# Compressed attention branch: two heads in one transposition and one weighted sum, with a block diagonal value matrix

## The chip, the cores and the metric

One core of a Trainium2 chip runs the whole kernel in one launch. The metric is the device time of one execution in microseconds (us). PE is TensorE, DVE VectorE, ACT ScalarE, Pool GpSimd, and SP is SyncE, which here only issues transfers.

## The reference

The kernel computes one decoder layer for 1024 tokens of width 1024 in float32: a normalised mixer with three families of heads (4 NSA heads, 8 sliding window heads with sinks, 4 stick-breaking heads), an output projection, and a gated feed-forward part. The change touches the first of three branches of the NSA heads, the compressed one:

```python
def nsa_compress(kv, pos, w1, b1, w2):          # 63 compressed keys or values of 64
    idx = jnp.arange(nc)[:, None] * 16 + jnp.arange(32)[None]
    blocks = (kv[:, idx] + pos).reshape(b, nc, 32 * d)
    return jax.nn.silu(blocks @ w1 + b1) @ w2

# per block of 128 queries, 4 heads, one shared set of compressed keys kc and values vc
lc = einsum('bhqd,bcd->bhqc', qb, kc) * scale + bias_tab[t5_bucket(dist_c)]
pc = masked_softmax(lc, dist_c >= 0)
o_c = einsum('bhqc,bcd->bhqd', pc, vc)
...
return g[0] * o_cmp + g[1] * o_slc + g[2] * o_win
```

In the sizes used every selection takes in all blocks, so the selected branch is full causal attention.

## The kernel before

The kernel runs in stages: projections, attention, output projection, feed-forward. Attention is cut into jobs of 128 queries by 4 heads: 8 stick-breaking jobs (`sb`), 16 sliding window jobs (`swa`), and then for each of 8 query blocks n a compressed (`cmp`), a window (`win`) and a selected (`slc`) job. "Compressed job n" below is that of block n; it sees L = 8n + 7 compressed keys, 7 to 63.

A job runs in these steps. `scores` (L980, L988): PE multiplies queries by keys, each number as a high and a low part. `logits` (L1390): DVE adds the bias, negates, and keeps the minimum of each row in `neg`. `softmax` (L1186): ACT takes the exponential; the rows lie in `rows_sb`, `rows_swa`, or `rows_nsa[kind]`, 128 queries on the partitions. `turn` (L1015): PE transposes 128 queries by up to 128 keys of each of the 4 heads into one PSUM bank. `keep` (L1216 on ACT or L1420 on DVE, whichever the plan finds free) copies that bank to one of three slots of `tw`. `weigh` (L1037): PE multiplies the turned weights by the values, 66 columns for each head (64 values and two ones, whose result is the sum of the weights), into bank `SUMS`. `combine` (L1443, L1446, L1450, L1456): DVE divides, multiplies by the gate and adds to the mix. The next job's first `weigh` waits for it. After a block's last job come squares on ACT (L1236), their mean on DVE (L1462), the root on Pool (L809), `norm_mix` on DVE (L1470), and the transposition of the mix (L1004).

In this float32 form each product is two PE instructions, a transposition is one. For a compressed job there are 4 transpositions of 128 x L and 4 products of L x 66; `VC` holds the values, 64 partitions of 66.

The order of all engines' work in attention is written out by `plan_attention`: a list scheduler that is given a cost for each step, what it needs and an age, and emits a fixed order for each engine. At run time semaphores guard each need. The last projection pieces (`piece`, L899) lie between the attention jobs, and the last one ends just before the first compressed logits, because `rows_cmp` shares its room with operands of the pieces. The gain of the NSA norm, `g_n`, has a tile of its own and is loaded by `("strip", 4)` (L746) after the last piece. Output weights are loaded and split (L1250, L1480) during attention.

## Time and profile before

| | before |
|---|---|
| median of 3 runs | 1280.15 us |
| lowest run | 1279.1 us |
| profiled execution | 1279.56 us |
| its span | 1277.8 us |
| PE busy | 1247.4 us (98%) |
| DVE busy | 869.9 us (68%) |
| ACT busy | 603.4 us (47%) |
| Pool busy | 251.4 us (20%) |
| mean granted TensorE clock | 0.990 |

The span runs from the first to the last instruction of the profiled execution; 1.8 us of its time lie around it. Busy shares are means over stages with different limits. PE's ends are modelled, so a busy PE may still have gaps.

### The profile page before, as it was taken

How to read it: one execution, taken by the hardware profiler on the slowest of the kernel's cores; microseconds unless marked ns; L12 is line 12 of the kernel's file. 1: busy time of each engine (PE TensorE's matmuls, PEld its weight loads, DVE VectorE, ACT ScalarE, POOL GpSimd, SP SyncE). 2: the span in 40 equal slices, each digit the busy share in tenths (PEclk: the TensorE clock that was granted, in tenths of full speed). 3: DMA queues.
4: the chain of work that ended last, by engine and by line, in shares of the span. 5: the costliest groups of instructions: out<-in, count | busy, mean ns of one | idle time of the engine just before them, and what ended most of it. 6: DMA issues, size and time to landing. Idle time of an engine off the chain costs nothing.

```text
span 1277.8 us, 19230 instructions
## 1 busy us (share of the span) xinstructions
PE 1247.4 (98%) x6792; PEld 1069.3 (84%) x6792; DVE 869.9 (68%) x1609; ACT 603.4 (47%) x1142; POOL 251.4 (20%) x198
## 2 busy tenths in 40 slices
PE   9999999999999999999999999999999999999997
PEld 7898878789989888888788888888888887788886
DVE  6323788768868666355976656656756659969875
ACT  6432677756657555343643333333333336544441
POOL 5230111110000000011001112111212137607113
PEclk9999999999979999999999999999999999999999
DMA  6303421147632000222312232233232367372433
GB/s 229 117 1 117 116 51 51 30 118 178 147 120 67 18 18 6 75 86 99 132 42 96 100 119 80 86 124 124 91 115 93 118 210 266 110 228 89 135 138 132
DMA packets 67172, 136.45 MB, mean 107 GB/s; under 512 B 8663, under 2 KB 27359, under 8 KB 67076
## 3 DMA queue, kind: packets, MB, share of 16 engines
q1 hardware_dynamic: 67076, 135.22, 33.9%
q8 instruction: 55, 0.90, 0.3%
q14 instruction: 41, 0.34, 0.1%
HBM read 89.81 MB, written 28.60 MB: 93 GB/s over the span
## 4 chain that ended last, share of the span: by engine, by line
PE 81%; DVE 9%; issue 4%; ACT 2%; POOL 1%; DMA 1%; SPq 1%; DVEq 0%; POOLq 0%; ACTq 0%
PE ps L2392 33%; PE ps L2422 13%; PE ps L1037 7%; PE ps L2336 6%; PE ps L1015 4%; PE ps L880 4%; PE ps L825 3%; PE ps L899 3%; PE ps L980 2%; PE ps L988 2%; DVE ring L1406 2%; PE ps L914 1%; DVE m_rows_sb L1413 1%; DMA m_qs<-m_qn 1%; DVE ring L1398 1%
## 5 line engine op out<-in xcount | busy, mean ns | idle before, releaser
L2392 PE MATMUL ps<-f_topH,f_W 128*128 128x512 f32 x704 | 220.4, 389 | 0.0
L2392 PEld LDWEIGHTS ps<-f_topH,f_W 128*128 128x128 f32 x704 | 132.2, 188 | 27.4
L2392 PE MATMUL ps<-f_topL,f_W 128*128 128x512 f32 x352 | 136.9, 389 | 0.0
L1037 PE MATMUL ps<-V,m_tw 128*128 128x66 f32 (+1 forms) x1056 | 130.2, 273 | 1.1 <-DVE m_mix_n L1450 1.1
L1037 PEld LDWEIGHTS ps<-V,m_tw 128*128 128x128 f32 x1056 | 127.7, 193 | 2.6 <-DVE m_mix_n L1450 1.5
L2422 PE MATMUL ps<-f_headH,f_W 128*128 128x512 f32 x408 | 128.5, 391 | 1.2 <-DVE QT L2217 1.1
L2392 PE MATMUL ps<-f_headH,f_W 128*128 128x512 f32 x352 | 116.1, 393 | 2.4 <-DVE f_p1a L2189 2.4
L2182 DVE TENSOR_TENSOR f_W<-f_scr,f_W 128x512 fp32r<-128x512 f32 x88 | 62.0, 708 | 79.0 <-ACT f_W L1967 78.9
L2182 DVE TENSOR_TENSOR f_W<-ring,f_W 128x512 fp32r<-128x512 f32 (+1 forms) x84 | 77.3, 929 | 42.5 <-ACT f_W L1967 42.4
L2422 PEld LDWEIGHTS ps<-f_headH,f_W 128*128 128x128 f32 x408 | 76.6, 188 | 18.0 <-issue 2.0
L1216 ACT COPY m_tw<-ps 128x512 f32<-128x512 f32 (+4 forms) x93 | 52.8, 583 | 66.3 <-PE ps L1015 36.1
L2392 PEld LDWEIGHTS ps<-f_headH,f_W 128*128 128x128 f32 x352 | 66.9, 190 | 16.6 <-issue 2.8
L2422 PE MATMUL ps<-f_headL,f_W 128*128 128x512 f32 x204 | 79.4, 389 | 0.0
L2392 PEld LDWEIGHTS ps<-f_topL,f_W 128*128 128x128 f32 x352 | 66.1, 188 | 13.7
L809 POOL TENSOR_TENSOR m_rs<-m_ms,m_mhalf 128x1 f32<-128x1 f32 x24 | 15.6, 648 | 277.2 <-DVE m_ms L1462 277.2
L2422 PE MATMUL ps<-f_b22H,f_W 128*128 128x512 f32 x208 | 66.9, 393 | 2.7 <-DVE QT L2217 1.9
L2392 PE MATMUL ps<-f_headL,f_W 128*128 128x512 f32 x176 | 69.2, 393 | 0.0
L2217 DVE TENSOR_TENSOR QT<-ps,QT 128x512 f32<-128x512 f32 x67 | 45.8, 684 | 28.9 <-PE ps L2422 28.8
L899 PE MATMUL ps<-m_hH,m_wH 128*128 128x512 f32 x144 | 59.6, 414 | 4.9 <-ACT QT L1118 4.8
L805 POOL TENSOR_TENSOR QT<-QT 128x512 f32<-128x512 f32 x24 | 34.8, 1462 | 148.6 <-ACT QT L1118 140.1
L2336 PE MATMUL ps<-o_w,o_mH 128*128 128x512 f32 x224 | 60.5, 392 | 0.0
L2392 PE MATMUL ps<-f_b22H,f_W 128*128 128x512 f32 x176 | 57.7, 389 | 0.0
(285 smaller groups left out, 2887.2 us busy)
## 6 DMA issues: line engine op xcount, KB each, us to landing
act_pairs<-QT SPq DMA_DIRECT2D x77, 256.0 KB, 4.1
f_stage<-act_pairs SPq DMA_DIRECT2D x77, 256.0 KB, 2.7
m_qs<-m_qn SPq DMA_DIRECT2D x128, 128.0 KB, 2.4
ring<-in_ffn_w_up SPq DMA_DIRECT2D x22, 512.0 KB, 3.7
ring<-in_ffn_w_gate SPq DMA_DIRECT2D x19, 512.0 KB, 4.6
ring<-in_w_in_tiles SPq DMA_DIRECT2D x9, 512.0 KB, 3.7
ring<-in_nsa_phi_w SPq DMA_DIRECT2D x8, 512.0 KB, 4.7
ring<-in_w_out SPq DMA_DIRECT2D x8, 512.0 KB, 5.0
```

Of the source, the lines that this page charges most:

```text
L805: pool.tensor_tensor(half_room(h), half_room(h), scale_row[:, half_cols(h)], ALU.mult).then_inc(half_scaled, 1)
L825: return pe.matmul(ps[:, h, :], w[:, k % W_ITEMS, (h // 2) * P:(h // 2 + 1) * P], a[:, k, half_cols(h)], start=first, stop=last)
L880: ins = pe.matmul(ps[:, b + a, 0:VW_HALF], h[:, k, tok], wv[:, w, k, a * VW_HALF:(a + 1) * VW_HALF], start=(k == 0 and h is hH and w == 0) ...
L899: ins = pe.matmul(ps[:, bank, :], w[:, n % W_ITEMS, cols], a[:, k, hf * HALF:(hf + 1) * HALF], start=(k == 0 and w is wH and a is hH), sto ...
L1015: ins = pe.transpose(ps[0:w, bank, i * P:(i + 1) * P], row_part(4 * j + i, slice(kb * P, kb * P + w)), ident[:])
L1037: ins = pe.matmul(ps[:, SUMS, wide * i:wide * (i + 1)], tw[0:w, t % W_SLOTS, P * i:P * i + P], v, start=(kb == 0 and i == 0), stop=(kb == ...
L1216: act.copy(out, src).then_inc(kept_by["act"], 1)
L2182: dve.tensor_tensor(slots[s % W_RING][:, 1, 0:n], source(s), slots[s % W_RING][:, 0, 0:n].bitcast(F32), ALU.subtract).then_inc(lo_done, 1)
L2217: dve.tensor_tensor(part, product_, part, ALU.add).then_inc(y_added, 1)
L2336: ins = pe.matmul(ps[:, 2 * (t % 2) + hf, :], m[:, t % 2, k, :], w[k][:, a, hf * HALF:(hf + 1) * HALF], start=(k == 0 and m is mH and a == ...
L2392: ins = pe.matmul(ps[:, bank, :], whole[:, w, cols], halves[h][:, k0 + k, col:col + HALF], start=(begins and k == 0 and w == 0 and h == 0) ...
L2422: ins = pe.matmul(ps[:, bank, :], whole[:, w, k * P:(k + 1) * P], block(n)[h], start=(begins and k == 0 and w == 0 and h == 0), stop=(k == ...
```

## The change

Heads are taken in pairs. The exponentials of two heads of a compressed job, each 64 columns wide with zeros after column L, lie side by side and are transposed in one step of 128 x 128: heads 0 and 1 in the first, 2 and 3 in the second. The turned weights of one head lie on partitions 0 to 63, those of the other on 64 to 127. `VC` becomes a block diagonal matrix of 128 x 132: the values and two ones at the upper left, the same at the lower right, zeros elsewhere. One product gives both heads' sums side by side. `keep` copies 256 columns in place of 512.

For this the unused columns of `rows_cmp` must be zero: Pool clears the tile once after the last piece (`cmp_zero`), and the compressed logits wait for it. `VC` is cleared and gets its ones at the start, and ACT copies the values into it twice. `g_n` loses its tile and shares `g_sb`, so its load waits for the last norm of the stick-breaking family instead of the last piece. The planner is given the new costs and steps.

```diff
@@ -260,7 +260,8 @@
     add(("strip", 0), "dma", 7000, [("turn", lay.last_turn(SB_JOBS - 1))], -100)
     for i in range(1, 4):
         add(("strip", i), "dma", (0, 5000, 5000, 7000)[i], [("scores", lay.chunk0[4 * SB_JOBS] - 1)], -100)
-    add(("strip", 4), "dma", 3000, [("piece", PIECES - 1)], -100)
+    add(("cmp_zero", 0), "pool", 400, [("piece", PIECES - 1)], -100)
+    add(("strip", 4), "dma", 3000, [("norm_mix", NT - 1)], -100)
 
     for j, job in enumerate(jobs):
         g = job.group
@@ -298,6 +299,8 @@
                     w = lay.width(c)
                     strip = ("strip", 0) if job.kind == "swa" else ("strip", 1 if job.n < 2 else 2 if job.n < 4 else 3)
                     rows_free = {"nsa": ("piece", PIECES - 1)}.get(job.family)
+                    if job.kind == "cmp":
+                        rows_free = ("cmp_zero", 0)
                     if job.kind == "slc" and job.n == 0:
                         rows_free = ("turn", lay.last_turn(SB_JOBS + SWA_JOBS - 1))
                     add(("logits", lay.c_sm[c]), "dve", dve(w), [("scores", c), used, strip, rows_free], age)
@@ -312,10 +315,11 @@
             at = lay.turn_at["w", t]
             bank_free = lay.same_bank_before[at]
             bank_free = [("keep", bank_free)] if bank_free is not None else [("half_keep", HALVES - 1)] if at >= lay.main_from else []
-            add(("turn", at), "pe", 440, [weights] + bank_free, age)
-            add(("keep", at), "any", act(HALF), [("turn", at), ("weigh", t - W_SLOTS) if t >= W_SLOTS else None], age)
+            few = job.kind == "cmp"
+            add(("turn", at), "pe", 220 if few else 440, [weights] + bank_free, age)
+            add(("keep", at), "any", act(HALF // 2 if few else HALF), [("turn", at), ("weigh", t - W_SLOTS) if t >= W_SLOTS else None], age)
             free = [combined(j - 1)] if t == lay.turn0[j] and j else [("half_keep", FIRST_HALVES)] if t == 0 else []
-            add(("weigh", t), "pe", 896, [("keep", at)] + free, age + 3)
+            add(("weigh", t), "pe", 496 if few else 896, [("keep", at)] + free, age + 3)
         age = 10.0 * j + 9
         last = ("weigh", lay.turn0[j + 1] - 1)
         n = job.n
@@ -474,7 +478,6 @@
         qn = sb("qn", [P, 2, 2, 2, P], F32R)
         tw = sb("tw", [P, W_SLOTS, HALF])
         mix_a = sb("mix_a", [P, 2, 512])
-        g_sb = sb("g_sb", [P, 256])
         junk = sb("junk", [P, HALF], mybir.dt.bfloat16)
         sink, neg_sink = sb("sink", [P, 8]), sb("neg_sink", [P, 8])
         neg, coef = sb("neg", [P, NR - 4 * SB_JOBS]), sb("coef", [P, NR - 4 * SB_JOBS])
@@ -482,6 +485,7 @@
         ss, ms, rs = (sb(n, [P, 3 * NT]) for n in ("ss", "ms", "rs"))
         ms0, rs0, neg_rs0 = sb("ms0", [P, NT]), sb("rs0", [P, NT]), sb("neg_rs0", [P, NT])
         mhalf = sb("mhalf", [P, NT])
+        g_sb = sb("g_sb", [P, 256])
         with ExitStack() as early:
             gain = sb("gain", [P, KT], F32, early)
             w2s = sb("w2", [P, 2, 2, HD], F32, early)
@@ -496,13 +500,13 @@
         kc2, vc2, scale_row = QT[:, 2, :], QT[:, 3, :], QT[:, 1, :]
         rows_nsa = {"slc": rows_slc, "win": sb("rows_win", [P, 4, WIN_BLOCKS * P]), "cmp": sb("rows_cmp", [P, 4, 64])}
         mix_n = sb("mix_n", [P, 2, 256])
-        g_n = sb("g_n", [P, 256])
+        g_n = g_sb
 
         ring_in = [sem(f"ring_in{i}") for i in range(RING)]
         x_in = keep["tile_in"]
         small_in, ext_oh_in = sem("small_in"), sem("ext_oh_in")
         consts_set, pool_set = sem("consts_set"), sem("pool_set")
-        ones_at, ident_at, ext_at, vones_at, kcs_at, masks_at, rs0_at = 1, 2, 3, 5, 6, 8, 9
+        ones_at, ident_at, ext_at, vc_zero_at, vones_at, kcs_at, masks_at, rs0_at, cmp_zero_at = 1, 2, 3, 5, 7, 8, 10, 11, 12
         pe_set, first_in = sem("pe_set"), sem("first_in")
         sums_at, scale_at, tab_at, kv_at = 1, 2, 3, 4
         squared_done, summed_done, token_step = sem("squared_done"), sem("summed_done"), sem("token_step")
@@ -601,6 +605,10 @@
         def row_of(r):
             return row_part(r, slice(0, jobs[r // 4].L))
 
+        def cmp_rows(a):
+
+            return rows_nsa["cmp"][:, 2 * a:2 * a + 2, :].rearrange("p h k -> p (h k)")
+
         def column(r):
             return r - 4 * SB_JOBS
 
@@ -633,13 +641,13 @@
                 return (QT[:, k0:k0 + n_k, t * P:(t + 1) * P], ps[:, bank, 0:n_k * P].rearrange("p (k q) -> p k q", k=n_k),
                         lambda eng: eng.wait_ge(q_lo, last_group(what, t) + 1))
             j = job_of_turn[t]
-            w = min(P, jobs[j].L - (t - turn0[j]) * P)
+            w = HALF if jobs[j].kind != "cmp" else HALF // 2
 
             def slot_free(eng):
                 if t >= W_SLOTS:
                     eng.wait_ge(weighed, t - W_SLOTS + 1)
 
-            return tw[0:w, t % W_SLOTS, :], ps[0:w, bank, :], slot_free
+            return tw[:, t % W_SLOTS, 0:w], ps[:, bank, 0:w], slot_free
 
         def wait_mix_free(eng, family, n):
             if n >= 2:
@@ -742,7 +750,7 @@
                     sp.wait_ge(tab_out, 32)
                     sp.dma_start(strip_swa[:], bass.AP(table_swa.tensor, 0, [[1, P], [SWA_T, 8], [1, SWA_L]])).then_inc(strips_in[0], 16)
                 elif i == 4:
-                    sp.wait_ge(piece_done, pieces(PIECES))
+                    sp.wait_ge(normed, NT)
                     sp.dma_start(g_n[:], bass.AP(grp_g.tensor, 0, [[0, P], [1, 256]])).then_inc(gains_in[2], 16)
                 else:
                     c0, c1 = STRIP_PARTS[i - 1]
@@ -781,7 +789,11 @@
             pool.memset(ext[32:33, :], -BIG).then_inc(pool_set, 1)
             pool.wait_ge(pool_set, ext_at)
             pool.memset(V[:, :, :, HD:HV], 1.0).then_inc(pool_set, 1)
-            pool.memset(VC[:, HD:HV], 1.0).then_inc(pool_set, 1)
+            pool.memset(VC[:], 0.0).then_inc(pool_set, 1)
+            for a in range(2):
+                pool.wait_ge(pool_set, vc_zero_at + a)
+                pool.memset(VC[64 * a:64 * a + 64, HV * a + HD:HV * a + HV], 1.0).then_inc(pool_set, 1)
+            pool.wait_ge(pool_set, vones_at)
             pool.memset(KCS[:].bitcast(F32), 0.0).then_inc(pool_set, 1)
             pool.memset(mask_raw[:], 0.0).then_inc(consts_set, 1)
             pool.wait_ge(consts_set, 3)
@@ -810,7 +822,11 @@
 
             for h in range(FIRST_HALVES):
                 half_scale(h)
-            work = {"half_scale": half_scale, "root": root}
+            def cmp_zero(_):
+                pool.wait_ge(piece_done, pieces(PIECES))
+                pool.memset(rows_nsa["cmp"][:], 0.0).then_inc(pool_set, 1)
+
+            work = {"half_scale": half_scale, "root": root, "cmp_zero": cmp_zero}
             for what, arg in plan["pool"]:
                 work[what](arg)
 
@@ -1010,10 +1026,9 @@
                             pe.wait_ge(stick_ready, n_sb[4 * j + 4])
                         else:
                             pe.wait_ge(weights_ready, n_sm[4 * j + 4])
-                    w = min(P, job.L - kb * P)
-                    for i in range(4):
-                        ins = pe.transpose(ps[0:w, bank, i * P:(i + 1) * P],
-                                           row_part(4 * j + i, slice(kb * P, kb * P + w)), ident[:])
+                    for i in range(2 if job.kind == "cmp" else 4):
+                        rows = cmp_rows(i) if job.kind == "cmp" else row_part(4 * j + i, slice(kb * P, kb * P + P))
+                        ins = pe.transpose(ps[:, bank, i * P:(i + 1) * P], rows, ident[:])
                 ins.then_inc(turned, 1)
 
             def weigh(t):
@@ -1027,14 +1042,13 @@
                 if kb == 0 and j:
                     wait_combined(pe, j - 1)
                 wait_kept(pe, lay.turn_at["w", t])
-                w = min(P, job.L - kb * P)
-                wide = HD if job.kind == "sb" else HV
-                for i in range(4):
+                wide = {"sb": HD, "cmp": 2 * HV}.get(job.kind, HV)
+                for i in range(2 if job.kind == "cmp" else 4):
                     if job.kind == "cmp":
-                        v = VC[0:w, :]
+                        v = VC[:]
                     else:
                         v = V[:, job.kb0 + kb, job.v_head + (i if job.kind == "sb" else 0), 0:wide]
-                    ins = pe.matmul(ps[:, SUMS, wide * i:wide * (i + 1)], tw[0:w, t % W_SLOTS, P * i:P * i + P], v,
+                    ins = pe.matmul(ps[:, SUMS, wide * i:wide * (i + 1)], tw[:, t % W_SLOTS, P * i:P * i + P], v,
                                     start=(kb == 0 and i == 0), stop=(kb == job.nb - 1), skip_group_check=True)
                 ins.then_inc(weighed, 1)
 
@@ -1167,7 +1181,8 @@
             act.wait_ge(pe_set, kv_at)
             act.wait_ge(pool_set, kcs_at)
             act.copy(KCS[0:64, 0:NC_CMP], ps[0:64, 5, 0:NC_CMP])
-            act.copy(VC[0:NC_CMP, 0:HD], ps[0:NC_CMP, 4, 0:HD]).then_inc(kc_hi, 1)
+            act.copy(VC[0:NC_CMP, 0:HD], ps[0:NC_CMP, 4, 0:HD])
+            act.copy(VC[64:64 + NC_CMP, HV:HV + HD], ps[0:NC_CMP, 4, 0:HD]).then_inc(kc_hi, 1)
 
             def query_hi(g):
                 job = jobs[first_row[g] // 4]
@@ -1378,6 +1393,7 @@
                     dve.wait_ge(turned, lay.last_turn(SB_JOBS + SWA_JOBS - 1) + 1)
                 dve.wait_ge(strips_in[0 if job.kind == "swa" else 1 if job.n < 2 else 2 if job.n < 4 else 3], 16)
                 if job.kind == "cmp":
+                    dve.wait_ge(pool_set, cmp_zero_at)
                     bias = strip_full[:, h, 0:16 * (L - 1) + 1:16][:, ::-1]
                 elif job.kind == "swa":
                     bias = strip_swa[:, h, 0:L][:, ::-1]
@@ -2668,7 +2684,7 @@
             keep["V"] = core.sb("V", [P, NT, 8, HV], F32, heads)
             keep["gate"] = core.sb("gate", [P, NT, 12], F32, heads)
             keep["KCS"] = core.sb("KCS", [P, HD], F32R, heads)
-            keep["VC"] = core.sb("VC", [HD, HV], F32, heads)
+            keep["VC"] = core.sb("VC", [P, 2 * HV], F32, heads)
             phi = ins["nsa_cmp_pos"], ins["nsa_phi_w1"], ins["nsa_phi_b1"], ins["nsa_phi_w2"][0]
             mix = mixers(nc, core, ins["x_rows"], ins["w_in_first"], ins["w_in_tiles"], ins["w_in_values"], ins["ln_attn_pre"], phi, ins["rel_bias"],
                          ins["bucket_onehot"], ins["swa_sinks"], ins["grp_norm_g"], ins["w_out"][0], ins["ln_attn_post"],
```

## Rows read from the trace of the kernel before

**Rows 1.** the page: the chain that ended last by engine
```profile
PE 81%; DVE 9%; issue 4%; ACT 2%; POOL 1%; DMA 1%; SPq 1%; DVEq 0%; POOLq 0%; ACTq 0%
```

**Rows 2.** windows: stretch; busy us of PE, PEld, DVE, ACT, POOL; clock; DMA
```profile
363.30:531.00 167.70, 162.61 (x1198) 150.07 (x1198) 108.92 (x433) 94.82 (x183) 6.86 (x10) 0.95 0.15 43
...
363.00:367.10 4.10, 2.45 (x16) 1.56 (x14) 3.43 (x15) 4.10 (x10) 1.59 (x1) 1.00 0.42 146
...
367.10:380.80 13.70, 13.20 (x62) 12.75 (x62) 9.99 (x47) 7.46 (x20) 0.00 (x0) 0.50 0.61 198
...
452.40:455.90 3.50, 3.50 (x19) 3.45 (x19) 1.81 (x11) 1.73 (x6) 0.00 (x0) 0.51 0.25 57
```

**Rows 3.** groups by shape on PE, 0 to 540 us (busy us, mean ns)
```profile
L1037 PE MATMUL ps<-VC,m_tw 39*128 39x66 f32 x8 | 1.1, 278 | 0.0
...
L1015 PE MATMUL ps<-ident,m_rows_cmp 128*39 128x128 f32 x4 | 0.6, 272 | 0.0
```

**Rows 4.** the chain, compressed job 4 and a later weighted sum (start, us, what)
```profile
429.13 1.76 PE ps L1015 x16
...
432.51 1.03 PE ps L1037 x8
...
444.90 0.84 PE ps L1037 x8
```

**Rows 5.** timeline of PE: f32 products of 512 columns, narrow score products
```profile
60.15 1.88 PE L866 MATMUL ps<-m_diag,m_ones 128*128 128x512 f32 x4
...
354.76 0.28 PE L980 MATMUL ps<-KCS,m_qs 128*128 128x64 f32 x1
354.88 0.28 PE L988 MATMUL ps<-KCS,m_qs 128*128 128x64 f32 x1
```

**Rows 6.** the chain, compressed job 0
```profile
366.87 0.68 DVE m_tw L1420
...
367.60 1.12 PE ps L1004 x4
...
370.26 1.90 PE ps L1037 x8
```

**Rows 7.** the chain, compressed job 1
```profile
379.52 0.85 PE ps L1015 x4
...
383.78 0.60 DVE m_tw L1420
...
385.04 0.43 DVE m_mix_n L1450
```

**Rows 8.** the chain, compressed job 7
```profile
506.95 0.47 ACT m_tw L1216
...
508.10 1.46 POOL m_rs L809
```

**Rows 9.** one line's instructions: ns min/median/max, first and last start (L1216)
```profile
L1216 ACT COPY m_tw<-ps x93: 561/585/622, 141.8 to 525.1; 128x512 f32<-128x512 f32 x87, 15x512 f32<-15x512 f32 x1, 23x512 f32<-23x512 f32 x1, 39x512 f32<-39x512 f32 x1
L1216 ACT COPY QT<-ps x18: 352/378/586, 154.8 to 533.5; 128x256 f32<-128x256 f32 x12, 128x512 f32<-128x512 f32 x6
```

**Rows 10.** timeline: a Pool fill, the last half's copy, the first compressed logits
```profile
2.13 0.33 POOL L786 MEMSET m_mask_raw<- 128x256 f32 x1
...
363.34 0.69 DVE L1303 SCALAR_TENSOR_TENSOR QT<-ps,QT 128x512 f32<-128x512 f32 x1 [0.61 <-PE ps L899]
...
363.95 0.15 DVE L1390 CUSTOM_DVE_ANT_0 m_rows_cmp<-ps,m_strip_full 128x7 f32<-128x7 f32 x1
```

**Rows 11.** SyncE: the gain load in time, then the first family's last norm
```profile
363.33 0.33 SPq L746 DMA_DIRECT2D m_g_n<-in_grp_norm_g  x1
...
L1470 DVE SCALAR_TENSOR_TENSOR m_mix_a<-m_mix_a,m_rs,m_g_sb x8: 457/476/1293, 148.9 to 280.2; 128x256 f32<-128x256 f32 x8
```

**Rows 12.** timeline of ScalarE around the copy of VC
```profile
126.83 0.21 ACT L1170 COPY VC<-ps 63x64 f32<-63x64 f32 x1
...
127.72 0.71 ACT L1180 CAST m_qn<-QT 128x256 fp32r<-128x256 f32 x2 [0.69 <-POOL QT L805]
```

## The prediction

> **What bounds the kernel now.** I began with the page: the chain of work that ended last is PE for 81% and DVE for 9% [rows 1]. The windows show where the change sits: the eight compressed jobs run between 363 and 531 us, PE is busy 162.6 of those 167.7 us, DVE 109 and ACT 95 [rows 2]. So this stage belongs to PE, but not wholly: at each compressed job one has to ask whether the chain runs through PE, or whether DVE or ACT ends last. I read the chain job by job for that. The reader should see three kinds. In job 4 the chain goes through four transposes within a row of sixteen and then through the weighted sum's eight PE instructions [rows 4]; jobs 2, 3 and 6 look the same, job 5 too. In jobs 0 and 1 the granted clock is 0.5, the 1.2 GHz level, from 367.1 to 380.8 us, after a stretch in which PE was busy only 2.45 of 4.1 us [rows 2]. In job 7 the chain runs through ACT, Pool and DVE, not PE [rows 8]. A second, short half-clock stretch at 452.4 us covers job 5's transposes [rows 2].
>
> **Part 1, transposes.** Four per job become two. Sixteen transposes take 1.76 us on the chain, 0.11 us each [rows 4], and a compressed one costs as much as a wide one: four are busy 0.6 us with a mean of 272 ns, so (0.6 - 0.27)/3 = 0.11 us apart [rows 3]. Two fewer save **0.22 us** per job at full clock. At half clock four take 0.85 us [rows 7], so two fewer save 0.43.
>
> **Part 2, weighted sum.** Four f32 products of 66 columns are eight PE instructions and take 0.84 us on the chain, 0.105 each [rows 4]; the compressed ones are (1.1 - 0.28)/7 = 0.117 apart [rows 3]. After the change there are two products of 132 columns, four instructions. No row has this shape, so I bound it. Below: what sets 0.105 us is not the columns, because score products of 64 columns start 0.12 us apart [rows 5], and f32 products of 512 columns start (1.88 - 0.59)/3 = 0.43 us apart, where 0.59 is the tail of one [rows 5], which is 0.84 ns a column; 66 columns would be 0.055, 132 are 0.111. If loading the weights hides behind the columns, an instruction costs the larger of 0.105 and 0.111: four cost 0.44 us, and **0.40 us** is saved. Above: if the load adds to the columns, it is 0.105 - 0.055 = 0.05 us, an instruction is 0.16, four are 0.64, and 0.20 is saved. And if only columns counted, 4 x 66 = 2 x 132 and nothing would be. I take 0.40: the 64-column product starts as late after the one ahead as a 66-column f32 product although it needs far fewer column passes, so there is a floor, and 132 columns lie just above it.
>
> The page on TensorE of the Trainium skill ("TensorE: Matmul & The Clock Gate", section "Back-to-back issue gap") gives for an isolated product a spacing proportional to its columns plus 2.5 ns, about 30 ns at 66 columns a pass. By that rule the weighted sum would gain nothing, and only part 1 would be left. This case's rows speak against it at these widths, since 64 columns are 0.12 us apart; the same section says that weight loads lift the spacing of narrow products, and with that the trace agrees.
>
> **Part 3, the copy of the transposed weights.** It moves 256 columns a partition where it moved 512. On ACT 585 ns become about 378 [rows 9], on DVE I scale likewise, 0.68 to about 0.42. It counts only where it is on the chain: jobs 0 and 7.
>
> **Job by job.** Job 0: the transposes are done while PE waits anyway, 0; the copy on DVE is on the chain, 0.68 us ahead of the PE work at 367.60 [rows 6], 0.26 saved; the weighted sum is 1.90 us on the chain at half clock [rows 6], of which eight steps of 0.21 are its own; half of them is 0.84. Together 1.1. Job 1: transposes 0.43; the weighted sum saves nothing, since DVE is the chain from there to 385.04 [rows 7]. Jobs 2, 3, 4 and 6: 0.22 + 0.40 = 0.62 each, 2.5 together. Job 5: transposes at half clock 0.43, sum at full clock 0.40, 0.8. Job 7: the sum isn't on the chain, ACT's copy of 0.47 us is [rows 8], 0.2 saved. Sum: 1.1 + 0.4 + 2.5 + 0.8 + 0.2 = **5.0 us**.
>
> **What is added.** The fill of the compressed rows runs on Pool once the last projection piece is done. A Pool fill of 128x256 took 0.33 us [rows 10]. The same event starts DVE's copy of the last half at 363.34 us, 0.69 us long, and the first compressed logits stand behind it on DVE at 363.95 [rows 10]. So the fill should land under that copy: 0, and 0.35 if that cover fails; behind the logits on DVE wait the mean squares, the root on Pool and the norm that PE turns at 367.60 [rows 6]. On Pool's own queue only roots stand behind the fill. The logits of 32 rows get one wait more. The trace shows no such wait alone; each lies between nothing and the length of the logits itself, 0.15 us [rows 10], 4.8 in all on DVE, which is 9% of the chain [rows 1], so 0 to 0.4: I take 0.2, since DVE's own waits vanish behind its copy there [rows 10]. The second copy of the value matrix costs ACT another 0.21 us at 126.8 us, where ACT then sits idle 0.69 us waiting for Pool [rows 12]: hidden, and 0.21 if not. Pool's fills at the start (one of 128x132, two of 2 columns, with waits on each other) come long before its first addition; 0, at most 0.6 of Pool time, by the 0.33 of the larger fill [rows 10].
>
> The gain load leaves SyncE's queue at 363.33 us, where it took 0.33 [rows 11], and goes to about 280.7, when the first family's last norm has read the shared tile [rows 11]. What is queued behind it there are the query transfers of the second family; it can hold one up by its own 0.33 us, or longer if the order puts it ahead of something that is ready sooner. What stood behind it at 363.33 are two gain vectors and an output weight, which nothing waits for closely. I take 0, with 0.4 at worst. Every tile after the value matrix moves by 264 bytes; no row prices an address, and I take 0. Added cost taken: **0.3 us**, range 0 to 1.7.
>
> **Order.** The costs fed to the planner change for all eight jobs, so the written order of all engines from the first compressed job can change. A job's saving can land where DVE is the chain, as in job 1, or an idle gap can close. I count 0.5 us off for this. Net: 5.0 - 0.3 - 0.5 = **4.2 us**. The profiled execution took 1279.56 us, span 1277.8 and 1.8 around it; that is 0.6 under the median of the runs shown, 1280.15, and 0.5 over the lowest, 1279.1. 1279.6 - 4.2 = 1275.4; I say 1275.5. After 531 us PE stays the chain through the output projection, so what is gained is kept.
>
> **Rivals.** *Columns decide.* The change does less than it says: the weighted sums stay at their time, and of the 5.0 us the transposes (0.4 + 0.9 + 0.4 = 1.7) and the copies (0.5) remain; less 0.8 leaves 1.4: 1278.2. For it: the work in columns is equal. Against: the floor of 0.105 to 0.12 us. *The order gives it back.* The new order puts DVE or ACT last at more jobs, as jobs 1 and 7 show now; half or more of the saving is gone: 1277 to 1280. *The slow clock shrinks.* The half-clock stretch of 13.7 us becomes like the short one of 3.5 us: PE's 10 us at half clock would save another 5: 1270.5. *Slower: the clock falls longer.* PE gets less to do right where it idles now, between 363 and 367 us, and at each job after. If one more stretch as long as 13.7 us is granted at 1.2 GHz, PE's 13.2 busy us [rows 2] would have been 6.6, and the loss of 6.6 exceeds 4.2: 1282. It decides from a loss of 4.2 us on, that is 8.4 us more at half clock; a short stretch costs 1.75 and doesn't turn the sign. For it: such a drop followed the last gap. Against: the gap grows by only a few tenths of a us.
>
> **How the numbers follow.** Forecast 55%, 1274 to 1277. Columns 10%, order 17%, shorter slow stretch 6%, slower by the clock 12%. The range 1270 to 1281.5 takes in the first four and leaves most of the last out, and also reaches to added costs of 1.7. About 2%, 26 us, is what a measurement of this kernel tells from no change; no case comes near it, so within 2% has 97%, faster 2%, slower 1% for what I don't see.
>
> **What the profile after would show.** Right: 16 transposes from the compressed rows and 32 PE instructions on the value matrix of 132 columns; four of these 0.44 us on the chain; a fill on Pool that ends before 364.0 us; the stage from 363 to 531 shorter by 4 us and every later stage as long as before. Wrong: 0.64 or more for those four instructions; logits that start after 364.1; another stretch at clock 0.5; DVE or ACT on the chain in jobs 2 to 6. It would be most wrong if the order changes much ahead of 363 us.

## The result, and the profile after

| | before | after |
|---|---|---|
| median, us | 1280.02 | 1268.26 |
| lowest to highest, us | 1279.1 to 1280.15 | 1266.87 to 1270.24 |
| profiled execution, its span | 1279.56, 1277.8 | 1267.51, 1265.7 |
| mean granted clock | 0.990 | 0.994 |

The ratio of the two is 0.9911 (95% interval 0.9893 to 0.9928). One run of the kernel before, of 1780 us, stands apart from all others: the range and the ratio leave it out, the median of 1280.02 counts it (without it, 1279.89). The forecast had the direction right and the size wrong: 4.2 us were expected, about 11 came, and 1268.3 lies 1.7 us under the range.

Where the 12.1 us between the two spans lie can be read from the ends of four stages in the profiled executions. The attention stage, from the last projection piece to the last weighted sum, took 164.5 us before and 155.2 after; what is ahead of it 362.9 and 362.5; output projection 89.7 and 89.7; feed-forward 652.4 and 652.0; and from PE's last product to the end 8.2 and 6.3. The difference arises in the attention stage, as forecast, and a tail of 2 us that nobody forecast comes on top. (The 0.4 us ahead of the stage say nothing: over the profiled executions of all kernels below, its start lies anywhere between 361.4 and 366.3 us.)

The page of the kernel after, its chain that ended last by engine, looks like the one of before [rows 1]:

```profile
PE 82%; DVE 9%; issue 4%; ACT 2%; POOL 1%; DMA 1%; SPq 1%; POOLq 0%; DVEq 0%; ACTq 0%
```

Windows of the kernel after (stretch; busy us of PE, PEld, DVE, ACT, POOL; clock; DMA): the attention stage, then the gap at the first compressed job, the long half-clock stretch and the short one, which answer to [rows 2]:

```profile
362.50:517.70 155.20, 150.21 (x1136) 140.35 (x1134) 104.76 (x423) 92.55 (x180) 5.56 (x9) 0.96 0.16 45
361.50:365.60 4.10, 2.97 (x16) 2.02 (x14) 3.16 (x15) 3.28 (x8) 1.32 (x2) 1.00 0.37 110
365.60:375.80 10.20, 9.89 (x46) 9.89 (x47) 9.27 (x43) 7.81 (x21) 0.45 (x1) 0.50 0.72 230
447.60:451.10 3.50, 3.50 (x20) 3.50 (x18) 2.44 (x14) 1.88 (x6) 0.07 (x1) 0.52 0.15 35
```

The stretch at 1.2 GHz is 10.2 us long where it was 13.7. The new instructions, grouped by shape on PE (busy us, mean ns), are as many as forecast, 32 and 16:

```profile
L1051 PE MATMUL ps<-VC,m_tw 128*128 128x132 f32 x32 | 6.1, 320 | 0.0
L1031 PE MATMUL ps<-ident,m_rows_cmp 128*128 128x128 f32 x16 | 3.3, 287 | 0.0
```

The other order can be seen in compressed job 4. The chain of the kernel after (start, us, what) runs through it on PE alone:

```profile
425.05 1.53 PE ps L1031 x14
426.58 0.55 PE ps L1051 x4
427.13 0.44 PE ps L1031 x4
427.56 0.18 PE ps L996
```

Before, sixteen transpositions of 1.76 us, then scores, then the weighted sum's eight [rows 4]; now fourteen of 1.53, the sum's four of 0.55 right behind, four more transpositions, and only then scores. So two things differ in this job: the work is 0.23 + (1.03 - 0.55) = 0.71 us less (0.62 was forecast, with 1.03 taken as 0.84), and the **order** is another: in the written order of PE the compressed sum now stands right after the third group of the window job's transpositions, ahead of the fourth group and of the window job's four scores. What followed in the chain of the kernel before, beyond the rows shown there, was not PE:

```profile
434.61 0.07 DVE m_rows_win L1390
434.67 0.42 issue
435.09 0.10 DVE m_neg L1390
...
435.87 0.36 issue
```

That path through DVE cost PE little, though: it ends at a wait of PE of 0.27 us at 440.00, and the kernel after has one of 0.28 us in the same place, at 435.69. Job 4 shows the other order, and not what it is worth.

Job 7 shows that, on DVE. Before, the chain went ACT 0.47, Pool 1.46 [rows 8], and on to DVE: the norm of the block before stood ahead of the compressed job's `combine` on DVE, the norm waited for Pool's root, and PE's next sum waited for the combine. Timeline of the kernel before (start, us, engine, line; in brackets the idle time ahead and what ended it):

```profile
509.65 0.49 DVE L1470 SCALAR_TENSOR_TENSOR m_mix_n<-m_mix_n,m_rs,m_g_n 128x256 f32<-128x256 f32 x1 [0.50 <-POOL m_rs L809]
...
510.45 0.42 DVE L1450 TENSOR_TENSOR m_mix_n<-ps,m_coef 128x256 f32<-128x256 f32 x1
...
510.93 1.11 PE L1037 MATMUL ps<-V,m_tw 128*128 128x66 f32 x8 [0.79 <-DVE m_mix_n L1450]
```

In the kernel after PE waits nowhere in job 7; its sum behind the window job's transpositions has no idle time ahead of it:

```profile
501.26 1.01 PE L1051 MATMUL ps<-V,m_tw 128*128 128x66 f32 x8
```

There the combine goes first, as here in job 4: its last step starts at 427.78, the norm at 428.27, and when PE comes to the next sum at 428.80 nothing is left to wait for:

```profile
426.42 0.71 PE L1051 MATMUL ps<-VC,m_tw 128*128 128x132 f32 x4
...
427.78 0.42 DVE L1466 TENSOR_TENSOR m_mix_n<-ps,m_coef 128x256 f32<-128x256 f32 x1
...
428.27 0.48 DVE L1486 SCALAR_TENSOR_TENSOR m_mix_n<-m_mix_n,m_rs,m_g_sb 128x256 f32<-128x256 f32 x1
...
428.80 1.00 PE L1051 MATMUL ps<-V,m_tw 128*128 128x66 f32 x8
```

Read by jobs, the start of the compressed transpositions of jobs 0 to 7 is earlier than before by 0.4, 2.6, 3.1, 3.1, 4.1, 5.4, 6.4 and 7.9 us (the first were at 365.36 and 364.93, the last at 504.78 and 496.86). Job 0 with its clock gives 2.1, job 1 0.5 and job 2 nothing; jobs 3 to 6 give 1.0 to 1.5 each where 0.62 or 0.8 were forecast, and job 7, from there to the last weighted sum, 1.8 where 0.2 was (22.6 us before, 527.4 - 504.78; 20.8 after, 517.7 - 496.86).

### The profile page after: what moved, and what is told of

It reads as the page before. It is cut to its first block, busy times and chain, and to the rows that moved or that the text cites. A ratio compares the mean times of both kernels' runs of the same rounds, so it can differ in the third digit from the quotient of the medians.

```text
span 1265.7 us, 19142 instructions
## 1 busy us (share of the span) xinstructions
PE 1236.4 (98%) x6744; PEld 1060.5 (84%) x6744; DVE 867.6 (69%) x1608; ACT 603.5 (48%) x1144; POOL 251.7 (20%) x201
## 4 chain that ended last, share of the span: by engine, by line
PE 82%; DVE 9%; issue 4%; ACT 2%; POOL 1%; DMA 1%; SPq 1%; POOLq 0%; DVEq 0%; ACTq 0%
PE ps L2408 32%; PE ps L2438 14%; PE ps L1051 8%; PE ps L2352 6%; PE ps L1031 4%; PE ps L896 4%; PE ps L841 3%; PE ps L915 3%; PE ps L996 2%; PE ps L1004 2%; DVE ring L1422 2%; PE ps L930 1%; DMA m_qs<-m_qn 1%; DVE m_rows_sb L1429 1%; DVE ring L1414 1%
## 5 line engine op out<-in xcount | busy, mean ns | idle before, releaser
L1231 ACT COPY m_tw<-ps 128x512 f32<-128x512 f32 (+1 forms) x96 | 53.2, 569 | 58.0 <-PE ps L1051 30.1
L2408 PEld LDWEIGHTS ps<-f_topL,f_W 128*128 128x128 f32 x352 | 66.1, 188 | 13.6
```

The costliest lines, as they stand in the source:

```text
L1231: act.copy(out, src).then_inc(kept_by["act"], 1)
L2408: ins = pe.matmul(ps[:, bank, :], whole[:, w, cols], halves[h][:, k0 + k, col:col + HALF], start=(begins and k == 0 and w == 0 and h == 0) ...
```

## How the runs are compared

Most differences below are of one to four microseconds, and one cause moves all kernels at once: how long the clock is at 1.2 GHz. It differs between runs of one and the same kernel. Each run comes with its mean granted clock, so the time at half clock is 2 x (1 - clock) x time. A least-squares fit over all 221 runs that have a clock, with a constant for each kernel and one common slope, gives **0.37 us** lost for each us at half clock (standard error 0.02, scatter of a run 1.2 us). "At equal clock" below is that constant less the kernel before's, with its standard error. It is a regression, and not itself an experiment, and each run's clock is known to 0.001 only, 2.5 us at half clock. The kernel before ran beside each of the four groups of kernels; at equal clock its means agree within 0.3 us, so the groups can be compared.

```
                 runs  mean us  us at half clock  at equal clock (error)
before            84   1278.9        27.2            0
after             10   1268.2        18.3           -7.4 (0.4)
order_new         12   1275.6        25.5           -2.7 (0.4)
work_new          11   1276.9        29.5           -2.9 (0.4)
added_only        12   1280.4        27.1           +1.5 (0.4)
products4          6   1270.6        21.2           -6.1 (0.5)
turns_twice        4   1267.6        15.2           -6.9 (0.7)
cost_rest          6   1269.5        24.1           -8.3 (0.5)
cost_job0          6   1272.8        20.4           -3.6 (0.5)
wait_once          6   1267.0        17.3           -8.3 (0.5)
fill               6   1266.5        13.5           -7.3 (0.6)
fill_old_order    10   1273.7        18.1           -1.9 (0.4)
fill_wait_once     6   1268.5        15.2           -6.0 (0.6)
fill_before       12   1277.2        21.5           +0.4 (0.4)
sum_late           6   1271.8        17.0           -3.4 (0.5)
sum_early         12   1275.5        30.0           -4.5 (0.4)
early_before      12   1278.4        26.9           -0.4 (0.4)
```

Two executions of the kernel after show what the slope stands for. The profile of its repetition, `after_again`, has this attention stage:

```profile
362.70:514.00 151.30, 145.01 (x1135) 134.27 (x1134) 104.04 (x423) 92.88 (x180) 5.56 (x9) 1.00 0.17 47
```

The same instructions took 151.3 us at full clock and 155.2 with 13.6 us at half clock: 3.9 / 13.6 = 0.29 us for one. A PE that never waited would lose 0.5.

## Experiments

**First question: the order or the work?** `order_new` is the kernel before with the new written order; `work_new` is the change with the old one.

```diff
 order_new, against before (L315 to L318)
+            few = job.kind == "cmp"
-            add(("turn", at), "pe", 440, ...
-            add(("keep", at), "any", act(HALF), ...
+            add(("turn", at), "pe", 220 if few else 440, ...
+            add(("keep", at), "any", act(HALF // 2 if few else HALF), ...
-            add(("weigh", t), "pe", 896, ...
+            add(("weigh", t), "pe", 496 if few else 896, ...
 work_new, against after: the same three lines back to 440, HALF, 896
```

> The instructions of the kernel before, written out in the order that the planner gives for the new costs; nothing of the pairing is done. Theory A (the written order is worth about as much as the saved work: the stage from 363 us lost 9.3 us where I had priced 5.0 of work): 4 to 6 us faster than before, about 1275. Theory B (the order is neutral and the work was under-priced): within 1 us of before, 1279 to 1280. Theory C (only the half-clock stretches differ): the difference to before follows the microseconds at clock 0.5, half of them each, and the order at full clock gives nothing.

> The changed kernel with the old costs given to the planner, so that all engines keep the order of before, apart from the fill and the moved gain load. Theory A: the priced work alone, 4 to 5 us faster than before, about 1275. Theory B: nearly the whole gain, 1268 to 1270. Theory C: as A, but with the half-clock stretch of 13.7 us still there.

Measured: 1276.25 us, 0.9980 (0.9965 to 0.9994) for the order alone, 1275.82 us, 0.9986 (0.9973 to 1.0000) for the work alone. At equal clock -2.7 and -2.9: the two together would be -5.6, and the whole change has -7.4. The order is a gain, not the loss of 0.5 that the prediction took, and 1.8 us (error 0.7) exist only with both. Windows of the stage in the two kernels, order_new first:

```profile
366.20:528.30 162.10, 158.29 (x1183) 146.87 (x1183) 106.15 (x423) 93.95 (x180) 5.38 (x8) 0.95 0.16 44
```

```profile
366.00:525.10 159.10, 152.10 (x1135) 140.28 (x1135) 105.71 (x424) 92.09 (x179) 6.47 (x9) 0.96 0.16 44
```

In work_new PE is busy 7.3 us less than before (152.10 against 159.41 in the same stage of the kernel before), yet the stage is only 5.4 us shorter: the rest stays as gaps. The kernel after is busy 150.21 us and 9.3 us shorter. Job 7 has the plainest of these gaps. In work_new the norm waits for Pool's root, the compressed job's combine stands behind the norm on DVE, and PE waits 1.4 us for it, its longest wait for a combine in the stage (us in total, times, longest):

```profile
507.34 0.48 DVE L1486 SCALAR_TENSOR_TENSOR m_mix_n<-m_mix_n,m_rs,m_g_sb 128x256 f32<-128x256 f32 x1 [0.50 <-POOL m_rs L821]
...
508.14 0.42 DVE L1466 TENSOR_TENSOR m_mix_n<-ps,m_coef 128x256 f32<-128x256 f32 x1
```

```profile
PE ps L1051 <- DVE m_mix_n L1466: 1.9, 3, 1.4
```

In job 7 of order_new and of the kernel after PE waits for nothing.

**The work by its parts.** `products4` keeps the paired transpositions and the wide tile, but takes four products of 66 columns, each over all 128 partitions, against the left or right half of the block diagonal; the two products of a pair read the same turned weights. `turns_twice` issues each of the two paired transpositions twice, into the same place.

```diff
 products4, against after
-                wide = {"sb": HD, "cmp": 2 * HV}.get(job.kind, HV)
-                for i in range(2 if job.kind == "cmp" else 4):
+                wide = {"sb": HD}.get(job.kind, HV)
+                for i in range(4):
...
-                        v = VC[:]
+                        v = VC[:, HV * (i % 2):HV * (i % 2) + HV]
...
 turns_twice, against after
-                        ins = pe.transpose(...)
+                        for _ in range(2 if job.kind == "cmp" else 1):
+                            ins = pe.transpose(...)
```

> The changed kernel with the weighted sum in four products of 66 columns over 128 partitions, eight instructions, in place of two of 132 columns; order, transposes and copies as in the changed kernel. If the floor of 0.105 us an instruction holds: the eight take 0.84 us on PE against 0.44, and the kernel is 2.5 to 3.5 us slower than the changed one, about 1271. If only columns count: no difference.

> The changed kernel with each transposition of a compressed job done twice into the same place, so four per job as before. By 0.11 us each, 0.22 a job: at most 1.8 us slower than the changed kernel, 1 to 1.8. Nearly nothing if the transposes lie under other waits.

Measured: products4 1270.78 us (0.9936, 0.9916 to 0.9956), 2.4 over the kernel after in the mean and 1.4 (0.6) at equal clock. The direction is as expected, the size smaller than the 2.5 to 3.5; by jobs, it is 0.33 to 0.44 us longer in each of jobs 3 to 7, as 0.40 each would have it. Its timeline on PE, job 4, beside that of `sum_late` (below), where the four instructions of 132 columns stand between two others on PE and nothing waits:

```profile
424.89 1.10 PE L1051 MATMUL ps<-VC,m_tw 128*128 128x66 f32 x8
425.83 0.60 PE L1031 MATMUL ps<-ident,m_rows_win 128*128 128x128 f32 x4
```

```profile
430.06 0.61 PE L1065 MATMUL ps<-VC,m_tw 128*128 128x132 f32 x4
...
430.51 0.60 PE L1045 MATMUL ps<-ident,m_rows_win 128*128 128x128 f32 x4
```

From the start of the sum to the start of what follows: eight of 66 columns take 0.94 us, 0.118 each; four of 132 take 0.45, 0.113 each. (In the kernel after itself the four take 0.37 to 0.55 us at full clock, job by job, according to what stands beside them.) An instruction of twice the columns costs the same, which is the floor that the prediction argued for. turns_twice: 1267.84 us (0.9912, 0.9898 to 0.9926), no difference from the kernel after that can be told (+0.5, error 0.7, in four runs); 1 to 1.8 us are not excluded. By jobs, in the profiled execution, it is 0.08 to 0.16 us longer in each of jobs 3 to 7, where 0.22 was expected.

The Trainium skill ("TensorE: Matmul & The Clock Gate", section "Back-to-back issue gap") says that in a stream of load and matmul pairs the spacing is set by both, and gives about 81 ns at 128 columns. These float32 rows agree that columns alone don't set it, but the spacing here is 0.11 us, at 66 columns as at 132.

**What the added parts cost alone.** `added_only` is the kernel before plus Pool's clearing of the compressed rows, the wait of the compressed logits on it, the second copy and the wider tile of values, the shared gain tile and the later gain load. Transpositions, products and costs stay. The clearing of `VC` and the ones of its second half, on Pool at the start, are not in it.

```diff
 added_only, against before
-    add(("strip", 4), "dma", 3000, [("piece", PIECES - 1)], -100)
+    add(("cmp_zero", 0), "pool", 400, [("piece", PIECES - 1)], -100)
+    add(("strip", 4), "dma", 3000, [("norm_mix", NT - 1)], -100)
...
+                    if job.kind == "cmp":
+                        rows_free = ("cmp_zero", 0)
...
-        g_n = sb("g_n", [P, 256])
+        g_n = g_sb
...
-                        v = VC[0:w, :]
+                        v = VC[0:w, 0:HV]
...
+            act.copy(VC[64:64 + NC_CMP, 0:HD], ps[0:NC_CMP, 4, 0:HD]).then_inc(kc_hi, 1)
...
+                    dve.wait_ge(pool_set, cmp_zero_at)
...
```

> The kernel before, in its own order, with the additions of the change alone: the fill on Pool, the 32 waits for it, the shared gain tile with its load moved, the wider value tile and its second copy; transposes, products and copies as before. By the price in the prediction: 0 to 0.5 us slower than before. If the additions hide a real cost that the saved work pays for: 1 us or more slower. If the shifted addresses are worth something (the last stores leave 0.5 to 0.8 us sooner in every kernel of the changed form): up to 2 us faster.

Measured: 1280.55 us, 1.0010 (0.9997 to 1.0023); +1.5 (0.4) at equal clock, but only +0.3 between the profiled executions (1279.89 and 1279.56). So the added parts cost something between 0.3 and 1.5 us, inside the range of 0 to 1.7 that the prediction gave and probably above the 0.3 that it took. With this, the work removed is -2.9 - 1.5 = **-4.4 us** (error 0.5), where the prediction's sum is 5.0. Not all of it need lie in the attention stage: in the profiled executions the tail behind PE's last product is 8.3 us in added_only and 7.2 in work_new, and no edit touches it (see the last section).

**Is it the wait?** `wait_once` lets only the first compressed row of job 0 wait for Pool; on DVE's in-order queue the others are covered by it.

```diff
-                    dve.wait_ge(pool_set, cmp_zero_at)
+                    if job.n == 0 and r % 4 == 0:
+                        dve.wait_ge(pool_set, cmp_zero_at)
```

> The changed kernel with the logits' new wait for the fill on the first of the 32 rows only. In the changed kernel job 0's four logits start 0.19 to 0.29 us apart, where they were 0.08 apart before, and the mean squares behind them start at 364.36 though the last piece ended 0.44 earlier. If the wait is the cause: the spacing returns to 0.08, 0.4 to 0.5 us gained at job 0, little elsewhere, 1267.5 to 1268. If it is the fill on Pool: no change.

Measured: 1267.19 us (0.9910, 0.9889 to 0.9931), -0.8 (0.6) at equal clock. That the wait costs time is not shown. The fill itself is hidden as forecast: Pool has it under DVE's copy, and then the four logits are spaced wider than the 0.08 us of the kernel before (363.95 to 364.20). The kernel after:

```profile
362.90 0.69 DVE L1318 SCALAR_TENSOR_TENSOR QT<-ps,QT 128x512 f32<-128x512 f32 x1 [0.61 <-PE ps L915]
362.93 0.31 POOL L827 MEMSET m_rows_cmp<- 128x256 f32 x1 [8.36 <-PE ps L915]
...
363.51 0.15 DVE L1406 CUSTOM_DVE_ANT_0 m_rows_cmp<-ps,m_strip_full 128x7 f32<-128x7 f32 x1
...
364.27 0.17 DVE L1406 CUSTOM_DVE_ANT_0 m_rows_cmp<-ps,m_strip_full 128x7 f32<-128x7 f32 x1
```

That is 0.76 us for three steps against 0.25. I took the wait for the reason; but in wait_once, where three of the four have none, the same steps still take 0.56 us (364.42 to 364.98). Most of the widening isn't the wait. What it is stays open.

**Which jobs' order?** The planner's new costs are given to job 0 alone, or to all but job 0.

```diff
 cost_rest (old costs for job 0), against after
-            few = job.kind == "cmp"
+            few = job.kind == "cmp" and job.n > 0
 cost_job0 (new costs for job 0 alone), against after
-            few = job.kind == "cmp"
+            few = job.kind == "cmp" and job.n == 0
```

> The changed kernel with the old costs for compressed job 0 alone, so that the written order of job 0 is that of before and the later jobs keep the new one. Theory A (the order's gain lies in the later jobs, where the weighted sum now stands ahead of the window's scores): as fast as the changed kernel at equal clock, 1268 to 1270. Theory B (it lies in job 0, where the sum now fills PE's gap and the clock falls for a shorter time): 3 to 5 us slower than the changed kernel, 1272 to 1273, with a half-clock stretch of 13.7 us.

> The changed kernel with the new costs for compressed job 0 alone; jobs 1 to 7 are planned with the old costs. Theory A: most of the order's gain is lost, 1272 to 1274. Theory B: as fast as the changed kernel, 1268 to 1270, with a half-clock stretch of 10 us or less.

Measured: cost_rest 1269.50 us (0.9930, 0.9916 to 0.9945), cost_job0 1272.90 us (0.9956, 0.9939 to 0.9973). At equal clock cost_rest has the whole gain (-8.3, the kernel after -7.4), cost_job0 hardly more than work_new (-3.6 and -2.9). So the order's gain is in jobs 1 to 7. Job 0's order acts on the clock instead: with it the time at half clock is 18.3 and 20.4 us, without it 24.1 and 29.5 (differences 5.8 and 9.1, errors 2.4 and 2.8). But it does so only together with the new work: order_new, with the new order and the old work, has 25.5 us, the kernel before 27.2 (difference 1.7, error 1.4).

**Is it the early sum?** In the orders the first lasting difference from job 4 on is the place of the sum and of the combine. `sum_late` takes the kernel after and moves in jobs 4 to 6 the sum and the fourth group of the window job's transpositions behind the fourth window score, and the combine behind the norm. `sum_early` makes the opposite move in work_new, `early_before` in the kernel before with its own instructions.

```diff
 sum_late, against after, on the finished order (t: the job's sum; third, fourth: groups of the
 window job's transpositions; behind: its fourth score)
+    for n in range(4, NT - 1):
...
+        for k in (("weigh", t), fourth):
+            if pe_list.index(k) < pe_list.index(behind):
+                pe_list.remove(k)
+                pe_list.insert(pe_list.index(behind) + 1 + (k[0] == "turn"), k)
+        k, norm = ("combine", lay.j_sm[j]), ("norm_mix", 2 * NT + n - 1)
+        if dve_list.index(k) < dve_list.index(norm):
+            dve_list.remove(k)
+            dve_list.insert(dve_list.index(norm) + 1, k)
 sum_early and early_before, against work_new and before
+    for n in range(4, NT - 1):
...
+        pe_list.remove(("weigh", t))
+        pe_list.insert(pe_list.index(third) + 1, ("weigh", t))
+        pe_list.remove(fourth)
+        pe_list.insert(pe_list.index(("weigh", t)) + 1, fourth)
+        k, norm = ("combine", lay.j_sm[j]), ("norm_mix", 2 * NT + n - 1)
+        dve_list.remove(k)
+        dve_list.insert(dve_list.index(norm), k)
```

> The changed kernel with one move of the new order undone by hand in compressed jobs 4, 5 and 6: PE's weighted sum stands behind the window job's four scores again, and DVE's combination behind the norm. Theory A (this move is what the order is worth in the later jobs): 1.5 to 2.5 us slower than the changed kernel, at equal clock. Theory B (the gain is spread over many small moves, those of jobs 1 to 3 first): less than 0.7 slower.

> The changed kernel in the order of before, with that one move made by hand in jobs 4, 5 and 6: the sum ahead of the window's scores, the combination ahead of the norm. Theory A: 1.5 to 2.5 us faster than the changed kernel in the order of before (1276.9), at equal clock, so 1274.5 to 1275.5. Theory B: less than 0.7 faster.

> The kernel before with the same move in jobs 4, 5 and 6 and nothing else: the order's part without the pairing. Theory A: 1 to 2 us faster than before. Theory B: no difference, under 0.5.

Measured: sum_late 1271.83 us (0.9945, 0.9929 to 0.9960), 3.4 over the kernel after and +4.0 (0.6) at equal clock. sum_early 1275.43 us (0.9970, 0.9957 to 0.9982), -1.6 (0.5) against work_new at equal clock, and 0.4 us less in the median. early_before 1278.26 us (0.9994, 0.9982 to 1.0006): nothing that the fit can tell (-0.4, error 0.4).

The 4.0 us of sum_late look like nearly all of the 4.5 that separate the kernel after from work_new, but they are not the same microseconds. The traces tell them apart. This is the time from the start of one compressed job's transpositions to the next one's, and for job 7 to the last weighted sum. A star marks a stretch with some half clock in it (0.3 to 6.8 us); without it, after and after_again agree within 0.01 us:

```
us              job 3    job 4    job 5    job 6    job 7
before          23.70    23.83*   26.63*   25.35    22.66
early_before    23.69    23.46    26.79*   25.05    22.67
order_new       23.62    23.08    25.11    24.67    21.60
work_new        23.38    22.93    24.66    24.62    22.46
sum_early       23.38    22.59    24.28    24.19    25.74*
after           22.71    22.56    25.55*   23.86    20.82
after_again     22.71    22.56    24.00    23.87    20.81
sum_late        22.71    24.05    25.50    25.31    20.83
```

From work_new to the kernel after, at full clock, the new order takes off 0.67, 0.37, 0.66, 0.75 and 1.65 us, 4.1 in all. The largest part is job 7, which none of the three moves touches; there PE's 1.4 us of waiting for the combine behind the norm are gone. (No run moved job 7's steps alone.) In jobs 4 to 6 the new order is worth 1.8 us, and sum_early alone gets 1.15 of them. Sum_late loses 4.4 us in the same jobs, over twice what they had gained: it doesn't take them back to the old order, it opens gaps that the old order didn't have. So the early sum is a part of the gain, the new order depends on it, and with four transpositions and eight products it is worth little. What else makes up the gain in jobs 3 to 6 wasn't isolated.

The trace of sum_late shows what its move costs in the new order. The window score at 428.55 can't start when PE reaches it, since DVE's logits, which leave the minima in `neg`, free its bank, and after the late sum PE stands still for the combine:

```profile
428.55 0.45 PE L1010 MATMUL ps<-m_KSa,m_qs 128*128 128x384 f32 x1 [0.57 <-DVE m_neg L1420]
...
431.12 0.42 DVE L1480 TENSOR_TENSOR m_mix_n<-ps,m_coef 128x256 f32<-128x256 f32 x1
...
431.59 1.11 PE L1065 MATMUL ps<-V,m_tw 128*128 128x66 f32 x8 [0.49 <-DVE m_mix_n L1480]
```

Over 424 to 500 us, what PE waited for (us in total, times, longest), sum_late first, then the kernel after, then work_new:

```profile
PE ps L1010 <- DVE m_neg L1420: 2.8, 7, 0.6
PE ps L1065 <- DVE m_mix_n L1480: 1.5, 3, 0.5
```

```profile
PE ps L996 <- DVE m_neg L1406: 1.0, 4, 0.3
```

```profile
PE ps L996 <- DVE m_neg L1406: 1.5, 6, 0.3
```

4.3 us of waiting in sum_late against 1.0, or 3.3 more, where the time differs by 3.4 to 4.0 us. In the new order, the early sum fills PE while DVE still works on the logits that free the bank of the window scores, and its own combine is done before the next sum asks for it. But work_new, in the old order, waits 1.5 us in this window and never for the combine.

**Is it the clock?** If the gaps of PE around job 0 bring the half-clock stretch, products without use in them should shorten it. The idle products' result isn't read. `fill`, `fill_old_order`, `fill_before` and `fill_wait_once` add seven to the kernel after, work_new, the kernel before and wait_once: four behind the last projection piece, three behind job 0's transpositions, on the identity and into the idle sum bank.

```diff
+            def fill(n):
+                wait_combined(pe, SB_JOBS + SWA_JOBS - 1)
+                for _ in range(n):
+                    pe.matmul(ps[:, SUMS, 0:P], ident[:], ident[:], start=True, stop=True)
...
+                if (what, arg) == ("piece", PIECES - 1):
+                    fill(4)
+                if (what, arg) == ("turn", first_cmp):
+                    fill(3)
```

> The changed kernel with seven idle products (14 PE instructions of 128 columns, 1.5 us) into the free sums bank: four right behind the last piece, three behind job 0's transpositions, where PE has gaps of 0.9 and 0.6 us. They add nothing to the result. If the clock falls because of PE's gaps there: the half-clock stretch at 366 us is shorter or gone, 10 us of it fewer, up to 4 us faster, 1264 to 1268. If the gaps aren't the cause: the stretch stays, and the time is 0 to 1 us longer.

> The changed kernel in the order of before, with the seven idle products in PE's gaps around job 0. The same kernel without them spent 29.5 us at half clock on the mean of its runs, and 1276.9 us. If PE's gaps there bring the clock down: 8 to 14 us fewer at half clock, 1272 to 1274. If the order of job 0 does something else to the clock: no fewer, 1277.

> The kernel before with the seven idle products in PE's gaps around job 0 and nothing else. In the changed kernel in the old order they took 11 us of half clock away and 3.2 us of time. If PE's gaps bring the clock down: 8 to 12 us fewer at half clock than the 26.6 of before, and 2.5 to 4 us faster. If not: the same, up to 1 us slower.

> The changed kernel with both edits, the idle products and the single wait. If they add up: 0.8 to 1.4 us from the wait and 2 from the clock, 1264 to 1266 and faster than either. If the wait was noise: as the kernel with the idle products, 1266 to 1267.

Measured: fill 1265.99 us (0.9907, 0.9886 to 0.9928), fill_old_order 1273.75 (0.9954, 0.9936 to 0.9971), fill_before 1277.18 (0.9988, 0.9976 to 1.0001), fill_wait_once 1268.08 (0.9915, 0.9896 to 0.9934). In each pair the mean time at half clock is lower: 18.3 to 13.5 (error of the difference 3.8), 29.5 to 18.1 (2.9), 27.2 to 21.5 (1.7), 17.3 to 15.2 (3.9). Only the second and the third are clear of scatter. The means moved by -1.7, -3.2, -1.7 and, against the direction, +1.5 us; the last pair has six runs each, and its two gains don't add. So with the old order the gaps are a part of the cause of the slow stretch, by some 11 us of half clock with the new work; in the kernel before I had expected more than the 5.7 that came. None removes it: in fill's profile a short stretch stays, with PE busy all through:

```profile
382.40:385.80 3.40, 3.40 (x13) 3.30 (x12) 2.99 (x11) 2.91 (x5) 0.00 (x0) 0.50 0.16 64
```

**The kernel after once more**, beside added_only and two of the fills:

> The changed kernel itself once more, for more runs beside these: 1268 to 1269, about 19 us at half clock on the mean.

Measured: 1268.43 us (0.9912, 0.9893 to 0.9931), the first result again. Its six runs lie beside fill's, 1265.99; their intervals overlap, and no version here is shown to be faster than the kernel after.

## Why the prediction was wrong in size

The means differ by 1278.9 - 1268.2 = 10.7 us. By the runs:

| term of the prediction | taken | the runs show |
|---|---|---|
| work removed | -5.0 | -4.4 (work_new less added_only) |
| added cost | +0.3, 0 to 1.7 | +1.5 by the fit, +0.3 in the profile |
| order | +0.5 | -2.7 alone, -4.5 on top of the work |
| clock | 0 (a rival of 6%) | -3.3 (8.9 us less at half clock x 0.37) |

**The step that failed is "Order".** The prediction said that the order of all engines could change, and then wrote 0.5 us off as a loss, without a row behind it. The new order is worth 4.5 us with the new work (-7.4 against -2.9), and the traces show 4.1 us of gain by it in jobs 3 to 7, 1.65 of them in job 7 alone. Rows could have hinted at it: the chain left PE at jobs 1 and 7 [rows 7, 8], and the trace around job 7's rows shows a combine that stands behind a norm's wait for Pool. The prediction read both as places where the saving is lost. Job 7 was a place where a combine ahead of the norm closes a gap of PE's. Job 1 wasn't: in the kernel after PE waits 1.3 us for a combine there, 0.3 before. Its rival on the order only looked the other way; the term needed a range with both signs, some 5 us wide.

**The second miss is the clock.** "The slow clock shrinks" was priced with 5 us for 10 us, 0.5 each, at 6%; the runs give 0.37 each, and 8.9 us fewer. Cost_rest and cost_job0 tie it to job 0's order, order_new shows that the new work is needed too, and two of the fills show gaps as a part of its cause. The prediction named the gap from 363 to 367 us and expected it to grow; in it PE is busy 2.97 of 4.1 us now, 2.45 before [rows 2]. The rival "slower by the clock" had the right place and the wrong sign.

**Right, by its own steps.** *Transpositions:* two fewer save 0.23 us in job 4, 0.22 forecast; done twice, they cost 0.08 to 0.16 a job. *Weighted sum:* four of 132 columns take 0.45 us where nothing waits, 0.44 forecast; the rival "columns decide" is out. The saving was sized too small all the same: the eight of 66 take 1.03 us in these jobs [rows 4], the prediction took 0.84 from a later sum, so that a job saves 0.48 to 0.67 us at full clock, and not 0.40. *Job 0:* 2.1 us came until job 1, 1.1 forecast; how the excess divides between clock and order wasn't taken apart. *Job 7:* with the new work in the old order it is 0.20 us shorter (22.66 to 22.46), as forecast; the rest of its 1.8 us is the order. *Fill of the rows:* it ended at 363.24, before 364.0 as asked, and under DVE's copy. *Second copy and Pool's fills at the start:* no sign of a cost, but a few tenths couldn't be seen, since the start of the attention stage scatters by 5 us between kernels. *Gain load:* it left SyncE at 296.9 us, and the query transfers ahead of it were not held. *Later stages:* as long as before within 0.4 us, so what attention gained was kept. *Not foreseen:* the tail, 1.9 us in the profiled executions, which no term above names and which is inside the differences that the table gives to work and order if it is in every execution.

## What to carry to other kernels

When a change feeds new costs to a planner, the order is a term of its own, with both signs; build the two halves apart, new order with old work and old order with new work, before explaining anything. A step that gets shorter is worth more where it can be put ahead of something that waits for another engine: look in the chain for steps that stand behind a wait they don't need. When a move is undone by hand, look whether it gives back the old gaps or makes new ones, before its price is called the move's worth. And compare runs at equal clock, or a difference of 3 us in 1270 is put down to the wrong edit.

## What the runs showed of the hardware

*The clock varies between executions of one program.* In the attention stage of the kernel after it was at 1.2 GHz for 13.6 us in one profiled execution and not at all in another, for 3.9 us of time. The Trainium skill ("TensorE: Matmul & The Clock Gate", section "What's actually happening") says that the number of slow matmuls varies from run to run of the same kernel, and the two traces agree. Seven products of no use went with 5.7 and 11.4 us less of slow time in two pairs; in two more, 4.8 and 2.1 us less may be scatter.

*An f32 instruction of 132 columns costs as much as one of 66* (0.113 and 0.118 us in a row), so in products this narrow it is their number that counts.

*A tail that shortened without an edit.* From PE's last product to the end 8.2 us pass in before and 8.3 in added_only, 6.8 to 7.2 in order_new, work_new, sum_early, early_before, fill_before and fill_old_order, and 6.3 to 6.4 in all ten others, cost_job0 among them. One of SyncE's last stores, before and then after:

```profile
1272.02 1.33 SPq L2606 DMA_DIRECT2D out<-e_xt_sums  x1
```

```profile
1261.79 0.56 SPq L2622 DMA_DIRECT2D out<-e_xt_sums  x1
```

The same store is issued in 1.33 and in 0.56 us, some 740 us behind the edited stage. That isn't the whole of it: work_new issues it in 0.56 us as well and has a tail of 7.2, and of the 1.9 us between before and after, 0.8 lie ahead of the last store's issue and 1.1 behind it. The tail is seen only in the profiled executions, one of each kernel (two of the kernel after, with 6.3 both times). Early_before has 6.8 and is not faster than before by more than 0.4 (0.4) at equal clock, so it is open whether the other runs have it, and its cause wasn't tried.
